# A hybrid decoder step on eight cores: x tiles 1 to 3 and the weights in one queue, K projected by 128-token tiles, the decode tile transposed by DMA

## The reference: what is computed

```
h = rmsnorm(x, norm_gain)
q, k, v, g_gla, gk_lr, u, b_gate, c_gate, g_conv = split(h @ w_in)      # 1024 x 3600
gk = log_sigmoid(gk_lr @ w_gk_up + b_gk) / 16                           # forget gate, rank 16
o  = gla(q / 8, k, v, gk, S0)            # 4 heads: S_t = diag(exp(gk_t)) S_{t-1} + k_t^T v_t, o_t = q_t S_t
o  = rmsnorm(o, gla_norm_gain) * silu(g_gla)
hc = c_gate * u                          # 512 channels, causal convolution of width 3
yc = b_gate * conv3(hc) * silu(g_conv)
y  = rmsnorm(x + concat(o, yc) @ w_out, final_norm_gain)
```

## Time and profile before

| | before |
|---|---|
| median of 3 runs | 316.15 us (315.95 to 316.32) |
| the profiled execution | 316.64 us |
| its slowest core (core 3), first to last instruction | 314.8 us |
| spans of the 8 cores | 311.6 to 314.8 us |
| PE busy on core 3 | 293.2 us (93%) |
| DVE, ACT, POOL busy | 227.2, 187.9, 85.3 us |
| mean granted TensorE clock | 0.992 to 0.996 |

### The profile page before, as it was taken

The page is one execution under the profiler, slowest core; times in us unless marked ns, Lnnn a source line. Parts: engine busy times, 40 slices in busy tenths (PEclk is TensorE's granted clock), DMA queues, the critical chain, the costliest instruction groups (busy, mean ns, idle before and its releaser), DMA issues.

```text
span 314.8 us, 6051 instructions; the slowest of 8 cores (311.6 to 314.8 us)
## 1 busy us (share of the span) xinstructions
PE 293.2 (93%) x1866; PEld 147.3 (47%) x1866; DVE 227.2 (72%) x380; ACT 187.9 (60%) x409; POOL 85.3 (27%) x91
## 2 busy tenths in 40 slices
PE   0399999999999999999999999999999999999990
PEld 0284444554445555654444444445444444454460
DVE  3455765899787758998955958699946628787654
ACT  1719535793674458658528748697329656545264
POOL 1995000142032224240256141003102530111061
PEclk9999999999999999999999999999999999999997
DMA  6999999999115043189996513824333211001506
GB/s 156 210 167 160 169 164 170 293 167 218 54 33 202 2 133 137 32 218 222 193 218 231 170 67 102 264 55 119 100 117 101 84 67 69 19 0 69 200 23 246
DMA packets 32143, 42.65 MB, mean 135 GB/s; under 512 B 13352, under 2 KB 22192, under 8 KB 31728
## 3 DMA queue, kind: packets, MB, share of 16 engines
q1 hardware_dynamic: 27072, 30.16, 32.8%
q0 software_dynamic: 4752, 11.77, 21.9%
q10 hardware_dynamic: 288, 0.35, 0.4%
HBM read 38.10 MB, written 10.95 MB: 156 GB/s over the span
## 4 chain that ended last, share of the span: by engine, by line
PE 87%; DMA 4%; ACT 3%; issue 3%; DVE 2%; SPq 0%; ACTq 0%; DVEq 0%
PE ps L656 47%; PE ps L666 18%; PE ps L828 8%; DMA idp_sb<-idp 2%; DMA X<-x_all 2%; PE ps L632 2%; PE ps L1022 2%; PE ps L652 2%; PE ps L902 1%; PE ps L895 1%; PE ps L751 1%; PE ps L877 1%; PE ps L891 1%; DVE hT L634 1%; PE ps L1177 1%
## 5 line engine op out<-in xcount | busy, mean ns | idle before, releaser
L656 PE MATMUL ps<-hT,w_in_bf 128*128 128x512 bf16 x752 | 172.8, 379 | 0.2 <-ACT f L771 0.2
L656 PEld LDWEIGHTS ps<-hT,w_in_bf 128*128 128x128 bf16 x752 | 71.9, 98 | 82.4 <-issue 3.0
L686 POOL TENSOR_TENSOR X<-X,fg_sb 128x1024 f32<-128x1024 f32 x14 | 33.0, 2359 | 87.5 <-ACT xs L591 47.8
L591 ACT ACTIVATE xs<-X 128x1024 bf16<-128x1024 f32 x29 | 30.5, 1051 | 20.1 <-DVE X L675 18.1
L643 ACT ACTIVATE f<-ps 128x512 f32<-128x512 f32 (+1 forms) x34 | 19.7, 582 | 27.5 <-PE ps L656 24.9
L666 PE MATMUL ps<-w_out_bf,mixC 128*128 128x512 bf16 (+1 forms) x136 | 35.7, 367 | 0.0
L666 PE MATMUL ps<-w_out_bf,mixG 128*128 128x512 bf16 (+1 forms) x136 | 33.2, 367 | 0.0
L675 DVE TENSOR_TENSOR X<-ps,X 128x512 f32<-128x512 f32 x28 | 18.6, 685 | 18.2 <-PE ps L666 18.2
L828 PE MATMUL ps<-w_v_bf,hT 128*128 128x512 bf16 x128 | 29.6, 379 | 0.0
L644 ACT ACTIVATE f<-f 128x512 f32<-128x512 f32 (+1 forms) x34 | 20.9, 618 | 1.7
L645 ACT ACTIVATE f<-f 128x512 f32<-128x512 f32 (+1 forms) x34 | 20.9, 614 | 1.3
(11 more groups left out here) (183 smaller groups left out, 438.6 us busy)
## 6 DMA issues: line engine op xcount, KB each, us to landing
X<-x_all SPq DMA_DIRECT2D x23, 512.0 KB, 5.6
y<-X SPq DMA_DIRECT2D x14, 512.0 KB, 2.7
w_in_bf<-w_in_l POOLq DMA_DIRECT2D x24, 256.0 KB, 20.7
w_out_bf<-w_out_l POOLq DMA_DIRECT2D x2, 1024.0 KB, 50.9
X<-gla_in SPq DMA_DIRECT2D x8, 256.0 KB, 5.4
gla_s<-X SPq DMA_DIRECT2D x8, 256.0 KB, 3.9
w_v_bf<-w_v_l POOLq DMA_DIRECT2D x1, 1024.0 KB, 22.4
X<-x_all POOLq DMA_DIRECT2D x2, 512.0 KB, 37.2
```

The lines of the kernel that those rows point to most:

```text
L591: op("act", lambda e: e.activation(out=junk.t[:], in_=src.t[:], func=AF.Square, accum_out=st.t[:, 0:1]), 1.15, [src.r], [junk.r, st.r], ke ...
L656: op("pe", lambda e: [e.matmul(out=bank.t[:], lhsT=w_in_bf[:, c, kc, :], rhs=hT.t[:, kc, :], start=(kc == 0), stop=(kc == KC - 1)) for kc ...
L686: op("pool", lambda e: e.tensor_tensor(out=xb.t[:], in0=xb.t[:], in1=fgb.t[:], op=ALU.mult), 2.4, [xb.r, fgb.r], [xb.r], key + 2, fill)
```

## The change

Five things are changed. (1) In item 0 only x tile 0 stays on SP. Tiles 1, 2 and 3 are issued from POOL between the weights, and nothing on POOL waits for tile 0 any more. The keys of tiles 1 to 3 (4.5, 6.3, 7.9) put them between the weight chunks; the constants `cbf` go behind K1. (2) K0 and K1 of item 0 are projected by tile, like G0 and G1. (3) The decode tile is transposed by DMA on SP (`raw`): DMA transpose, then the gain in place on DVE. (4) In the last tile, the product of the first half with the final gain goes to a buffer of its own, `pf`. (5) The plan gets other numbers: `DMA_BEGIN` 5.3 for 12.0, other landings for x, a soft time for `nbgk`, and `ENDGAME`, by which operations with keys from 303 on, PE's excepted, are ordered by the length of the work behind them.

```diff
-    DMA_BEGIN = 12.0
+    DMA_BEGIN = 5.3
+    ENDGAME = 303.0
...
+        tail = {}
+        for o in reversed(self.ops):
+            d = min(o.alts.values(), key=lambda a: a[1])[1]
+            tail[o] = d + (o.bytes / self.RATE + self.DMA_LAT if o.bytes else 0.1) + max([tail[q] for q in o.succ] or [0.0])
+        for o in self.ops:
+            if o.key >= self.ENDGAME and "pe" not in o.alts:
+                o.key = self.ENDGAME + 30.0 - tail[o]
...
-            op("act", lambda e: e.mul(out=nbgk.t[:], in_=prm_t[:, PO_BGK:PO_BGK + 2], mul=-1.0), 0.2, [prm.r], [nbgk.r], 8)
+            op("act", lambda e: e.mul(out=nbgk.t[:], in_=prm_t[:, PO_BGK:PO_BGK + 2], mul=-1.0), 0.2, [prm.r], [nbgk.r], 8, soft=9.0)
...
-            dma("pool", lambda e: e.dma_start(out=cbf.t[:, 128:CBW], in_=cb_d[:, 128:CBW]), cb2, [], [R_cb], 6, 320 * KB, after=x_ops[0:1])
+            dma("pool", lambda e: e.dma_start(out=cbf.t[:, 128:CBW], in_=cb_d[:, 128:CBW]), cb2, [], [R_cb], 9.5, 320 * KB)
...
-                hold = x_ops[0:1] if k else ()
+                hold = ()
...
-            early = 512 <= r0 < 1024 and key < 60
+            early = 0 < r0 < 1024 and key < 60
...
+            if raw:
+                hv = lambda: hT.t[:, :, t * 128:(t + 1) * 128]
+                dma("sp", lambda e: e.dma_start(out=hv(), in_=xs.t[:], transpose=True), _Tslot(hT, t), [xs.r], [hR], key, 1024 * KB)
+                op("dve", lambda e: e.tensor_tensor(out=hv(), in0=hv(), in1=g_b, op=ALU.mult), 1.15, [hR, prm.r], [hR], key)
+                return
...
+            pf = FT.new(2)
...
-                    op("dve", lambda e, q=q: e.tensor_tensor(out=xb.t[:, Q[q]], in0=xb.t[:, Q[q]], in1=fgb.t[:, Q[q]], op=ALU.mult), 0.4,
-                       [xb.R[q], fgb.r], [xb.R[q]], key + 0.1 * q)
+                    op("dve", lambda e, q=q: e.tensor_tensor(out=pf.t[:, Q[q]], in0=xb.t[:, Q[q]], in1=fgb.t[:, Q[q]], op=ALU.mult), 0.4,
+                       [xb.R[q], fgb.r], [pf.R[q]], key + 0.1 * q)
...
-            op("act", lambda e: e.activation(out=xb.t[:, 0:512], in_=xb.t[:, 0:512], func=AF.Copy, scale=acc.t[:, 8:9]), 0.6,
-               [xb.R[0], xb.R[1], acc.R[8]], [xb.R[0], xb.R[1]], key + 1)
+            op("act", lambda e: e.activation(out=xb.t[:, 0:512], in_=pf.t[:], func=AF.Copy, scale=acc.t[:, 8:9]), 0.7,
+               [pf.R[0], pf.R[1], acc.R[8]], [xb.R[0], xb.R[1]], key + 1)
...
-                xb = x_load(r0 + t * 128, kl if i else 0.1 * t, kl if i else 0.0, {2: NG, 3: FG}.get(t) if i == 1 else None)
+                xb = x_load(r0 + t * 128, kl if i else (0.0, 4.5, 6.3, 7.9)[t], kl if i else 0.0, {2: NG, 3: FG}.get(t) if i == 1 else None)
...
-                bank = inproj(C_K + p, hT, p0 + 6 + 2 * p)
+                bank = inproj(C_K + p, hT, p0 + 6 + 2 * p, i == 0)
...
-            x_prep(xb, hTs, hTs.r, 0, base - 10)
+            x_prep(xb, hTs, hTs.r, 0, base - 10, False, True)
```

More of the change, by code:

```diff
@@ L560, in load_weights @@
             cb2 = _Slot(cbf.t, "cb2")
-            dma("pool", lambda e: e.dma_start(out=cbf.t[:, 128:CBW], in_=cb_d[:, 128:CBW]), cb2, [], [R_cb], 6, 320 * KB, after=x_ops[0:1])
+            dma("pool", lambda e: e.dma_start(out=cbf.t[:, 128:CBW], in_=cb_d[:, 128:CBW]), cb2, [], [R_cb], 9.5, 320 * KB)
             for k, c in enumerate(seq):
                 key = 0.5 if k == 0 else 2 + 1.7 * k
-                hold = x_ops[0:1] if k else ()
+                hold = ()
                 if c == "lr":
                     dma("pool", lambda e: e.dma_start(out=w_lr_bf[:].rearrange("p k n -> p (k n)"), in_=w_lr_d), B_wlr.slot,
-                        [], [B_wlr.r], key, 128 * KB, cost=0.65, land=5.6)
+                        [], [B_wlr.r], key, 128 * KB, cost=0.65)
                 elif c == "v":
@@ L583, in x_load @@
             xb = (home or X).new()
-            early = 512 <= r0 < 1024 and key < 60
+            early = 0 < r0 < 1024 and key < 60
             x_ops.append(dma("pool" if early else "sp", lambda e: e.dma_start(out=xb.t[:], in_=x_all[r0:r0 + 128, :]), _Late(xb), [], [xb.r], key, 600 * KB,
-                             land=(7.4, 9.0, 11.5, 13.5)[r0 // 128] if r0 < 512 and key < 1 else None, rel=0.0 if early else rel, cost=0.65 if early else 0.5, after=x_ops[0:1] if early else ()))
+                             land=7.2 if key == 0 else None, rel=0.0 if early else rel, cost=0.65 if early else 0.5, after=()))
             return xb
@@ L613, in get, with x_prep @@
                 return t_slots[k]
-        def x_prep(xb, hT, hR, t, key, by_dma=False):
+        def x_prep(xb, hT, hR, t, key, by_dma=False, raw=False):
             xs = XS.new()
```

## The result

The changed kernel took 319.43 us (median of 4 runs, 319.13 to 320.62) against 316.24 us of the kernel before beside it (315.95 to 316.65): 3.2 us slower, ratio 1.0111, 95% interval 1.0088 to 1.0134. The forecast was slower by 1.25 us. Its profiled execution, the longest of the four, took 320.62 us, with a span of 317.9 us on core 3 (314.8 before).

A forecast was written before the change was run, and what follows sets the result against it. PE was taken as the bound outside the start and the end. Start +1.6, decode tile -0.45 and end +0.1 gave +1.25 us: 317.4 us against 316.15, own range 316.8 to 318.2, whole range 315.3 to 318.6.

The forecast's parts named there:

- the start costs 29.1 - 27.5 = 1.6 us: Start: Q0's first matmul, by a worked list of PE, moves from 27.5 to 29.1 us, 1.6 us later.
- Landings: Start, POOL queue: G0 at 9.9 us, then x tiles 1, 2, 3 at 11.4, 14.6, 17.8; tile 0 at 7.55.
- The pace: Start: TensorE goes from 1.2 to 2.4 GHz at 20.9 us, where before it was about 20.0.
- the third wait: Start: PE waits 1.0 us, until 22.7, for `hT` of tile 2 ahead of its low-rank group.
- The base: Start of Q0 in the kernel before, taken as 27.49 us from the profile.
- Decode, -0.45: Decode tile: its eight PE transposes leave PE, which is the bound there, saving 0.45 us.
- The end, +0.1: Last tile: SP's last store 0.24 us earlier, the 1024-wide operation's store 0.45 later; taken as +0.1 us.
- the early pace: Rival, start: 2.4 GHz at about 17 us, Q0 at 27.4, time 315.8 us; chance 0.25.
- the better supply: Rival, start: tile 0 at 5.6, G0 at 9.3, full pace at 19.5; no change, 316.2 us; chance 0.15.
- Tile 0 was not held up: Rival, start: tile 0 shares DMA engines, lands at 8.8 to 9.2; 318.3 us; chance 0.12 with late decode tile.
- the decode transpose was not late: Rival, decode tile: its DMA transpose comes late, up to +1.5 us on top, 318.9; shares the 0.12 chance.
- the faster pair's middle: Early pace alone (315.8 us) and with earlier queue and tile 0 (315.1), taken as 315.2 for the pair; chance 0.25.

The follow-up runs named there:

- e6: Changed kernel plus 42 matmuls nobody reads, 18 ahead of PE's first transpose and 24 in its waits: 319.07 us against 317.66 before, ratio 1.0046.
- e8: Changed kernel with its queue part undone (x tiles on SP, weights held for tile 0) and added matmuls keeping PE busy: ratio 0.9990 to the kernel before.
- e11: Kernel before with only the decode tile transposed by DMA: ratio 1.0001 (0.9982 to 1.0020).
- e16: Changed kernel without the ordering by length of work behind, buffer `pf` kept: no ratio; 8.4 us from PE's last matmul to the end.
- e4: Changed kernel with x tiles 1 to 3 back on SP, weights still released at once from POOL: 320.14 us, ratio 1.0102 to the kernel before.
- e5: Changed kernel plus 18 matmuls nobody reads ahead of PE's first transpose: ratio 1.0057 to the kernel before.
- e1: Changed kernel with its queue part undone (x tiles on SP, weights held for tile 0, old plan numbers): 316.37 us against 316.61 before, ratio 0.9985.

## Why the prediction was wrong

The direction was right, and so was the place: the start. The step that failed is "**the start costs 29.1 - 27.5 = 1.6 us**"; it measured 3.1 on the mean of the cores and 3.7 on core 3, half to three quarters of it late landings and the rest the slow pace (e6 to e8). Three of its inputs were off.

*Landings.* "In queue order that gives tile 1 at 11.4, ... tile 2 at 14.6, ... tile 3 at 17.8". They landed at 12.2, 14.9 and 18.8 on the mean. I had the step between two tiles right on the whole (3.2 us; 2.7 and 4.0 measured), and G0, from which I counted, 0.5 early (10.4 in place of 9.9). I had also forecast tile 0 at 7.5 and PE's start at 10.2. With no other x tile beside it, tile 0 landed at 5.3 and PE started at 8.1 on core 3 (5.6 and 8.5 on the mean); those 2 us were won and lost again, because tile 1 sets what comes next. The Trainium skill, page "DMA: Bandwidth & Descriptors", section "Anatomy of one DMA — SWDGE (gpsimd) path", has about 2.0 us fixed for a GpSimd DMA. Here the low-rank weights, the first on POOL and 64 KB, took

```profile
DMA to landing us min/median/max: 4.1/4.1/4.1
```

and G0 behind them 8.2, so I was right to count by the rows.

*The pace.* "I let the full pace come as much later, at 20.9". It came at about 22.7 on the mean (19.4 before) and at 27.0 on core 3. The 20.9 was counted from a full pace at 20.0 before, and that is misread: 19.06 and 1.7 groups of 0.85 make 20.5. In the list any moment up to 22.7 gives the same Q0, because of the third wait, so this cost nothing, and the pace was too early for the slowest core alone. My own list, run with the landings measured on core 3 and the full pace at 27.0, gives 31.3, where Q0 was 31.2; with the full pace at 20.9 it gives 29.6. So on the slowest core this one number is 1.7 of the 2.1 us that I missed. I let one wait set the moment, but PE had five waits between 9 and 23 us, G1's landing with 1.9 us among them, which I had at nothing. What sets the moment stays open: core 1, with 2.4 us of waits for weights and the same three for `hT`, had the full pace at 23.6.

*The base.* 27.5 is core 3's Q0 before, with its tile 0 at 7.55. The mean was 26.1. My 29.1 met the mean core of the changed kernel (29.2) and I set it against the slowest core of the kernel before. It met it in part by luck: it was counted from core 3's tile 0, and with the mean landing of tile 0 before (6.2) my list gives about 28.5, an estimate, which tile 1's 0.8 us make good again. On equal terms the list would by that estimate have said +2.4 and not +1.6.

What held: two of the waits of 1.5 us for `hT` and the third (0.6 us on core 3, up to 1.0 on others); by-tile groups at 0.85 beyond 20 us; no wait for V, nor for the decode tile. Its transpose was issued at 93.7 and took 3.8 us to land, the gain ran at 101.3, later than I said and 1.88 us long, and PE came at 104.3:

```profile
L639 SPq DMA_TRANSPOSE hTs<-xs x1: 2457/2457/2457, 93.7 to 93.7; - x1
```

*Decode, -0.45.* PE's transposes behind 32 us take 1.79 us in place of 2.23, and from Q0 to PE's last matmul it is 0.7 less; e11 can't tell the gain from none, and of the 0.45 no run shows anything in time.

*The end, +0.1.* It was +0.4. I had moved the 1024-wide operation and its store, and not looked at ACT's list. The end of core 3, which answers to the earlier trace rows:

```profile
311.25 0.40 ACT L721 ACTIVATE xs<-hT 128x256 bf16<-128x256 f32 x1
...
311.65 0.67 ACT L727 ACTIVATE acc<-acc 128x1 f32<-128x1 f32 x2
...
312.79 0.20 ACT L732 ACTIVATE acc<-acc 128x1 f32<-128x1 f32 x1
313.09 0.72 ACT L737 ACTIVATE hT<-f,acc 128x512 f32<-128x512 f32 x1
313.45 0.75 DVE L734 SCALAR_TENSOR_TENSOR hT<-hT,acc,fg_sb 128x512 f32<-128x512 f32 x1 [0.85 <-ACT acc L732]
```

Both small sums now stand behind the last square, 0.67 where one of 0.28 stood, and DVE's half starts 0.46 us behind the scale, not 0.10. The first is the order by the length of the work behind: e16, without it, has one sum of 0.28 there. For the second no row names a cause.

Of the rivals, the early pace and the better supply fell. Tile 0 was not held up, and the decode transpose was not late. One slip stands in the sums: the faster pair's middle is called 315.2 and, in the range, 315.3, where 315.8 and 315.1 make 315.45.

## What to carry to other kernels

At a bandwidth-bound start the order in which bytes land is the schedule: put what opens work for PE (here all four tiles) ahead of what only continues it, whichever queue issues it, and keep a hold that enforces this, or put the order into one queue. Where the order of the engines is fixed ahead, it has to fit those landings (e4). An earlier first matmul is worth nothing when the second tile moves back. And compare a forecast list with the same statistic of the kernel before, mean core with mean core, above all where a clock that comes at its own time adds a spread of some us.

## What the runs showed of the hardware

2.4 GHz had been reached by 8.7 us in e5; then waits of 1.5 and 2.5 us with 0.7 us of work between them were followed by 1.2 GHz up to 23.6 us (granted clock 0.57 from 12 to 24). In these runs the column of the granted clock shows the slow pace only after such a fall. In the changed kernel, where by-tile groups took 0.89 us each up to 26 us, it says 1.00 (core 3, 12 to 24 us), so the pace has to be read from the matmuls:

```profile
12.00:24.00 12.00, 7.61 (x77) 6.54 (x78) 5.32 (x6) 4.66 (x12) 9.99 (x18) 1.00 1.05 198
```

42 matmuls that nobody reads removed the slow stretch on all eight cores and made them alike: Q0 within 0.4 us in place of 3.1 (e6). And with two open queues the bytes of both flow together: a tile issued 0.16 us behind a weights' DMA of the other queue landed 3.8 us later than in the run in which the weights were held (e4, e1).
